# A hybrid attention and mLSTM layer: rotated rows copied from SBUF to SBUF, and two of seven mLSTM operands split as their heads finish

## The reference, cut to what matters

```python
h = rmsnorm(x, norm_w)
q_a, k_a, v_a, z_a, q_m, k_m, v_m, o_m, z_m, g = split(h @ w_in)     # w_in: 2048 x 8208
# group A: 8 heads of 128; QK norm, rotary on the first 32 of 128 head dims,
qa = rope_partial(rmsnorm(q_a, q_norm_w)); ka = rope_partial(rmsnorm(k_a, k_norm_w))
# three (window, dilation) patterns, mixed by their softmax denominators
attn = mix(dilated_attention(qa, ka, va)) * silu(z_a)
# group B: 4 heads (qk 128, v 256), bidirectional chunked mLSTM
hm = rmsnorm(mlstm(qm, km, vm) + flip(mlstm(flip(...))), m_norm_w)
hm = sigmoid(o_m) * hm * silu(z_m)
y = x + concat([attn, hm]) @ w_out                                    # w_out: 2048 x 2048
```

## Time and profile before

| | us |
|---|---|
| median of 3 runs | 1972.75 |
| lowest, highest | 1968.98, 1974.37 |
| profiled execution | 1969.88 |
| its span, first to last instruction | 1968.1 |
| PE busy | 1920.2 (98% of the span) |
| DVE busy | 1354.8 (69%) |
| ACT busy | 896.3 (46%) |
| POOL busy | 226.5 (12%) |

### The profile page before, as it was taken

One profiled execution on the slowest core, in us unless ns is written; L12 is line 12 of the kernel. 1 busy time (PEld: TensorE's weight loads), 2 busy tenths in 40 slices (PEclk: granted clock), 3 DMA queues, 4 the chain that ended last, 5 costly groups with the idle time before them and its releaser, 6 DMA issues.

```text
span 1968.1 us, 26806 instructions
## 1 busy us (share of the span) xinstructions
PE 1920.2 (98%) x8865; PEld 1571.3 (80%) x8865; DVE 1354.8 (69%) x2804; ACT 896.3 (46%) x1494; POOL 226.5 (12%) x244
## 2 busy tenths in 40 slices
PE   8999999999999999999999999999999799999999
PEld 6888887788888888888887878778787687877787
DVE  7677868778768767867866565655665856557655
ACT  6554326335336425434444245546546464455222
POOL 0231000110010010011000211110110111111111
PEclk9999999999999999999999999999999899999999
DMA  6676544564464486366356963563655736447554
GB/s 212 219 266 224 196 143 147 134 149 132 119 164 128 106 230 180 102 147 152 122 190 263 242 162 86 137 162 64 174 120 144 257 75 193 112 108 216 100 120 105
DMA packets 164216, 310.09 MB, mean 158 GB/s; under 512 B 18224, under 2 KB 41408, under 8 KB 160976
## 3 DMA queue, kind: packets, MB, share of 16 engines
q1 hardware_dynamic: 131200, 243.36, 37.8%
q0 software_dynamic: 30720, 57.69, 18.7%
q10 hardware_dynamic: 2160, 7.34, 1.0%
HBM read 202.53 MB, written 122.56 MB: 165 GB/s over the span
## 4 chain that ended last, share of the span: by engine, by line
PE 84%; DMA 6%; issue 4%; DVE 3%; ACT 2%; SPq 0%; POOL 0%; DVEq 0%; ACTq 0%; POOLq 0%
PE ps L870 22%; PE ps L874 21%; PE ps L872 21%; PE ps L1043 3%; PE ps L1072 3%; DMA arena<-rot_dram 2%; DMA rot_dram<-arena 2%; PE ps L1012 1%; PE ps L968 1%; PE ps L977 1%; PE ps L1054 1%; PE ps L971 1%; PE ps L1044 1%; PE ps L889 1%; PE ps L1074 1%
## 5 line engine op out<-in xcount | busy, mean ns | idle before, releaser
L870 PE MATMUL ps<-t_hi,w_hi 128*128 128x512 f32 x2184 | 878.5, 402 | 23.4 <-issue 10.7
L874 PE MATMUL ps<-t_hi,w_lo 128*128 128x512 f32 x2184 | 854.4, 391 | 0.0
L872 PE MATMUL ps<-t_lo,w_hi 128*128 128x512 f32 x2184 | 853.8, 391 | 0.0
L870 PEld LDWEIGHTS ps<-t_hi,w_hi 128*128 128x128 f32 x2184 | 412.1, 189 | 115.9 <-issue 34.5
L874 PEld LDWEIGHTS ps<-t_hi,w_lo 128*128 128x128 f32 x2184 | 411.6, 188 | 88.3
L872 PEld LDWEIGHTS ps<-t_lo,w_hi 128*128 128x128 f32 x2184 | 412.3, 189 | 81.8
L1410 DVE TENSOR_TENSOR w_lo<-s_tmp,w_hi 128x512 fp32r<-128x512 f32 x312 | 221.3, 709 | 183.3 <-ACT w_hi L1109 173.1
L1109 ACT CAST w_hi<-s_tmp 128x512 fp32r<-128x512 f32 x312 | 193.0, 619 | 281.0 <-PE ps L874 263.8
L1410 DVE TENSOR_TENSOR w_lo<-w_raw,w_hi 128x512 fp32r<-128x512 f32 x234 | 165.2, 706 | 152.1 <-ACT w_hi L1109 146.1
L1109 ACT CAST w_hi<-w_raw 128x512 fp32r<-128x512 f32 x234 | 144.8, 619 | 222.1 <-PE ps L874 215.9
L455 POOL DMA_DIRECT2D fin_dram<-xt x32 | 28.1, 877 | 845.4 <-ACT xt L1128 812.6
(11 more groups left out here) (226 smaller groups left out, 2292.4 us busy)
## 6 DMA issues: line engine op xcount, KB each, us to landing
w_raw<-w_all_dram SPq DMA_DIRECT2D x320, 256.0 KB, 4.1
fin_dram<-xt SPq DMA_DIRECT2D x128, 256.0 KB, 4.4
fin_dram<-xt POOLq DMA_DIRECT2D x128, 256.0 KB, 5.5
arena<-fin_dram SPq DMA_DIRECT2D x64, 512.0 KB, 7.6
outT_dram<-xt POOLq DMA_DIRECT2D x60, 256.0 KB, 4.3
arena<-xT_dram SPq DMA_DIRECT2D x44, 256.0 KB, 5.7
arena<-xT_dram SPq DMA_DIRECT2D x16, 512.0 KB, 4.5
outT_dram<-xT_dram SPq DMA_DIRECT2D x16, 512.0 KB, 5.7
```

Of the source, the lines that this page charges most:

```text
L870: nc.tensor.matmul(ps[:, bank, :], hi, t_hi[:, n, k, :], start=new and k == 0, stop=False, skip_group_check=True)
L872: nc.tensor.matmul(ps[:, bank, :], hi, t_lo[:, n, k, :], start=False, stop=False, skip_group_check=True)
L874: mm = nc.tensor.matmul(ps[:, bank, :], lo, t_hi[:, n, k, :], start=False, stop=k == KP - 1, skip_group_check=True)
```

## The change

There are two parts.

**Rotated rows.** POOL's store to and load from `rot_dram` go. SP now copies the rotated rows from `turn` straight into raw q or k, in four transfers of 32 partitions x 256 elements for each of the two, at `at` 5 (q) and 6 (k), ahead of the broadcast of that step. To do so SP waits for DVE's rotation (`a_rot`).

**Two operands split early.** Operands 0 and 2 of the mLSTM half of y are plain blocks: the first 512 columns of heads 0 and 1, and of heads 2 and 3. At `at` 61 of each mLSTM head ACT copies those columns of `gate` to `yk_hi`, at 62 DVE makes `yk_lo`, and at 63 SP stores both in `yk_dram`. They lie where `hbuf` lies, so the next head's first result waits for the store, and the load of block B21 for the border at 329 moves from offset -9 to -4, its scaling on ACT from -5 to 0. At the border at 441 ACT loads both parts of operands 0 and 2 from `yk_dram`, and their two splits are gone; the split of operand 3 moves from offset 8 to 7 and that of 4 from 9 to 8.

```diff
-Y_SPLIT = {3: {3: 0, 5: 1, 6: 2, 8: 3, 9: 4, 10: 5, 11: 6}, 4: {3: 0, 5: 1, 6: 2, 7: 3, 8: 4, 9: 5, 10: 6}}
+Y_SPLIT = {3: {5: 1, 7: 3, 8: 4, 10: 5, 11: 6}, 4: {3: 0, 5: 1, 6: 2, 7: 3, 8: 4, 9: 5, 10: 6}}
+Y_KEPT = (0, 2)
...
+        yk_hi = nc.alloc_sbuf_tensor_at("yk_hi", [P, 2, HALF], F32R, offset=arena_at + 4 * 2048)
+        yk_lo = nc.alloc_sbuf_tensor_at("yk_lo", [P, 2, HALF], F32R, offset=arena_at + 4 * 3072)
...
# SP, loads of the border at 329, and its wait
-                if off == -9 and b == 2:
+                if off == -4 and b == 2:
                     sp.wait_ge(m_htr, 2 * M_HEADS)
+                    sp.wait_ge(yk_out, 32 * M_HEADS)
-                for blk, at in ((B11, -13), (B12, -12), (B22, -11), (B21, -9)):
+                for blk, at in ((B11, -13), (B12, -12), (B22, -11), (B21, -9 if b == 1 else -4)):
...
# SP, mLSTM head j
                 if at == 25:
                     if j > 0:
                         sp.wait_ge(m_out, 16 * j)
+                        sp.wait_ge(yk_split, 2 * j)
...
+                if at == 63:
+                    sp.wait_ge(yk_split, 2 * j + 2)
+                    n, kp = divmod(2 * j, KP)
+                    for part_, src in enumerate((yk_hi, yk_lo)):
+                        sp.dma_start(yk_dram[n, part_][:, kp:kp + 2, :], src[:].bitcast(F32)).then_inc(yk_out, 16)
...
# SP, attention head h
                 if at in (5, 6):
                     i = at - 5
+                    sp.wait_ge(a_rot, 8 * h + 4 * i + 4)
+                    sp.wait_ge(a_sq, 2 * h + 2)
+                    for part_ in range(4):
+                        k, q = divmod(part_, 2)
+                        sp.dma_start((raw_a, raw_b)[i][0:ROT, part_ * 256:(part_ + 1) * 256],
+                                     turn[i][2 * ROT * k + q:2 * ROT * (k + 1):2, 0:256]).then_inc(turned[i], 16)
                     sp.wait_ge(rs_out, 32 * (h + 1))
...
# ACT
-                for blk, at in ((B11, -10), (B12, -9), (B22, -8), (B21, -5)):
+                for blk, at in ((B11, -10), (B12, -9), (B22, -8), (B21, -5 if b == 1 else 0)):
...
+                if at == 61:
+                    act.wait_ge(m_y, 2 * j + 2)
+                    nc.scalar.copy(yk_hi[:], gate.rearrange("p (e t) -> p e t", e=2)[:, :, 0:HALF]).then_inc(yk_split, 1)
...
-                    y_there(act, 3, off - 1)
-                    act.dma_start(t_lo[:, off - 1].bitcast(F32), y_block(3, off - 1)).then_inc(t_in[off - 1], 16)
+                    if off - 1 in Y_KEPT:
+                        act.wait_ge(yk_out, 32 * M_HEADS)
+                        for part_, t in enumerate((t_hi, t_lo)):
+                            act.dma_start(t[:, off - 1].bitcast(F32), yk_dram[Y_KEPT.index(off - 1), part_]
+                                          ).then_inc(t_in[off - 1], 16)
+                    else:
+                        y_there(act, 3, off - 1)
+                        act.dma_start(t_lo[:, off - 1].bitcast(F32), y_block(3, off - 1)).then_inc(t_in[off - 1], 16)
...
# DVE
                     if n == 0 and j > 0:
                         dve.wait_ge(m_htr, 2 * j)
+                        dve.wait_ge(yk_out, 32 * j)
...
+                if at == 62:
+                    dve.wait_ge(yk_split, 2 * j + 1)
+                    nc.vector.tensor_tensor(yk_lo[:], gate.rearrange("p (e t) -> p e t", e=2)[:, :, 0:HALF],
+                                            yk_hi[:].bitcast(F32), ALU.subtract).then_inc(yk_split, 1)
...
-                dve.wait_ge(turned[i], 16 * (h + 1))
+                dve.wait_ge(turned[i], 64 * (h + 1))
...
# POOL: gone
-                    pool.wait_ge(a_rot, 8 * h + 4 * i + 4)
-                    pool.dma_start(rot_dram[h, i], turn[i][:, 0:256]).then_inc(rot_out[i], 16)
...
-                    pool.wait_ge(rot_out[i], 16 * (h + 1))
-                    pool.wait_ge(a_sq, 2 * h + 2)
-                    pool.dma_start(halves((raw_a, raw_b)[i][0:ROT]),
-                                   rot_dram[h, i].rearrange("(s r q) n -> r s (q n)", s=2, q=2)).then_inc(turned[i], 16)
```

More of the change, by code:

```diff
@@ L138 @@
 SUMS = (3, 1, 5, 4)
+Y_KEPT = (0, 2)
 FIRST_SPLIT = (4, 1, 4, 1, 1, 5, 4)
 def t_made(n, b):
-    return FIRST_SPLIT[n] + b - int(b >= 2 and n in KEPT)
+    return FIRST_SPLIT[n] + b - int(b >= 2 and n in KEPT) - int(b >= 3 and n in Y_KEPT)
 def t_loaded(n, b):
-    return 32 * (n in KEPT) + 16 * (b - 2)
+    return 32 * (n in KEPT) + 16 * (b - 2) + 16 * (b >= 3 and n in Y_KEPT)
 def sums_of_y(h):
@@ L168, in prepared_in, with build_program @@
     return u + 2 if u + 2 < UNITS else None
-def build_program(nc, xT, w_all, w_gates, vecs, norm_cols, m_cols, att_mask, rope, eye, tri, fin, xrs_dram, y_dram, t_dram, ty_dram, eps_dram, rows_dram, rs_dram,
-                  rot_dram, outT):
+def build_program(nc, xT, w_all, w_gates, vecs, norm_cols, m_cols, att_mask, rope, eye, tri, fin, xrs_dram, y_dram, t_dram, ty_dram, yk_dram, eps_dram, rows_dram, rs_dram, outT):
     with ExitStack() as ctx:
@@ L377, in build_program @@
         m_out = sem("m_out")
+        yk_split = sem("yk_split")
+        yk_out = sem("yk_out")
         q_raw = sem("q_raw")
@@ L391, in build_program @@
         turn_in = [sem(f"turn_in{i}") for i in range(2)]
-        rot_out = [sem(f"rot_out{i}") for i in range(2)]
         a_rot = sem("a_rot")
@@ L863, in product @@
                     pe.wait_ge(t_in[n], t_loaded(n, 2))
+                elif g == STAGE[3] and n in Y_KEPT:
+                    pe.wait_ge(t_in[n], t_loaded(n, 3))
                 elif g in STAGE:
@@ L2042, in squares @@
                         nc.gpsimd.tensor_tensor(sq_acc, sq_acc, x_ring[:, r % 2, :], ALU.add).then_inc(xg_sum, 1)
-            def turned_rows(h, at):
-                if at in (4, 5):
-                    i = at - 4
-                    pool.wait_ge(a_rot, 8 * h + 4 * i + 4)
-                    pool.dma_start(rot_dram[h, i], turn[i][:, 0:256]).then_inc(rot_out[i], 16)
-                if at in (5, 6):
-                    i = at - 5
-                    pool.wait_ge(rot_out[i], 16 * (h + 1))
-                    pool.wait_ge(a_sq, 2 * h + 2)
-                    pool.dma_start(halves((raw_a, raw_b)[i][0:ROT]),
-                                   rot_dram[h, i].rearrange("(s r q) n -> r s (q n)", s=2, q=2)).then_inc(turned[i], 16)
             def add_ym(u):
@@ L2072, in _ @@
                 added(*divmod(u, PRODUCTS))
-                for h in range(ATT_HEADS):
-                    turned_rows(h, u - A_START[h])
                 add_ym(u)
@@ L2188 @@
     rs_dram = nc.dram_tensor("rs_dram", (ATT_HEADS, 2, TB, P), _mybir.dt.float32, kind="Internal").ap()
-    rot_dram = nc.dram_tensor("rot_dram", (ATT_HEADS, 2, P, 256), _mybir.dt.float32, kind="Internal").ap()
     eps_dram = nc.dram_tensor("eps_dram", (2 * TB, P), _mybir.dt.float32, kind="Internal").ap()
@@ L2193 @@
     ty_dram = nc.dram_tensor("ty_dram", (2, len(SUMS), P, KP, HALF), _mybir.dt.float32, kind="Internal").ap()
+    yk_dram = nc.dram_tensor("yk_dram", (len(Y_KEPT), 2, P, KP, HALF), _mybir.dt.float32, kind="Internal").ap()
     outT = nc.dram_tensor("outT_dram", (O_TILES, P, SEQ), _mybir.dt.float32, kind="ExternalOutput").ap()
-    build_program(nc, *args, fin, xrs_dram, y_dram, t_dram, ty_dram, eps_dram, rows_dram, rs_dram, rot_dram, outT)
+    build_program(nc, *args, fin, xrs_dram, y_dram, t_dram, ty_dram, yk_dram, eps_dram, rows_dram, rs_dram, outT)
     r = _run(nc, [arrays], core_ids=[0])
```

## The result

The changed kernel takes 1980.72 us (median of 20 runs, 1973.49 to 1986.43), the kernel before 1974.38 us in the same comparison (20 runs, 1968.55 to 1986.56). The ratio is 1.0026, with a 95% interval of 1.0014 to 1.0038: slower by about 5 us (2.8 to 7.5). Forecast were 1963.7 us and a range of 1956 to 1971; the time is outside it and on the other side of before.

The account below looks back on a forecast made before the run. PE was taken as the bound, busy 1920.2 of 1968.1 us, with gains only where it waits. The terms -6.6 - 3.4 + 0 + 0.3 + 0.6 = -9.1 us took 1972.75 to 1963.7 us, range 1956 to 1971.

Parts of the forecast that it names:

- The other edits: Step pricing mLSTM's added copy and subtraction at 0.3 us, and the border at 329 at +0.6 us.
- bound of 4.9 us: Upper limit for the mLSTM work: the time each of DVE and ACT would add if nothing hid it.
- signs of being wrong: Listed observations that would refute the forecast, among them new PE waits at the last steps of an mLSTM head.
- The border at 441: Removing operand 2's split resumes PE 2.3 us earlier, but the gain moves to another wait: 0, bounds -4 and +3.
- upper bound of +3: At the border at 441, operand 2's second megabyte delays the broadcast in a crowded stretch; 1 MB is 2.9 us.
- what is late next?: Question at the border at 441, answered by head 5's broadcast: issued no earlier, with four copies now before it.
- The rotated rows: Attention heads: an 8.9 us path after rotation replaces POOL's round trip, saving 6.6 us of waits and 3.4 of clock.
- two clock windows: After the waits of heads 0 and 7, PE's full clock returns: 2 x 1.7 = 3.4 us saved.
- Rival 1: Attention heads: copies ahead cost the broadcast 2 us of landing; only -2.0 us in all, 1970.7 us; chance 0.21.
- The rule of turns between queues: On SP: DMA engines take queues in turn, so copies ahead in its queue make the broadcast land later; no separate size.
- The border at 329: B21's four scalings, 2.56 us on ACT, now just before the first cast: +0.6 us, bounds 0 and 2.6.
- Rival 2: Attention heads: broadcast landings of 9.8 us become the rule, making it 22.9 us slower, 1995.6 us; chance 0.07.

Follow-up runs that it names:

- ym_late: Changed kernel with the first three steps of the copies of y moved from units 226, 231, 236 to 246, 251, 256; 1967.91 us, 0.9993 of before.
- store_late: Changed kernel with head 1's store of kept parts moved from step 63 to 68, behind head 2's k and q loads; 1969.16 us, 0.9990 of before.
- border_thin: ym_late with all but 64 columns of operand 2's low part not loaded at the border at 441; 1965.49 us, 0.9965 of before.
- rot_only: Kernel before with only the rotated rows moved to SP, no operands kept; 1966.24 us, 0.9981 of before.
- rot_swap: rot_only with SP issuing each step's broadcast ahead of the four copies; 1960.37 us, 0.9954 of before; repeated, 1960.18 us, 0.9935.
- store_act: Changed kernel with all four heads' stores of kept parts issued by ACT instead of SP at step 63; 1977.84 us, 1.0019 of before.

## Why the prediction was wrong

**The step that failed: "The other edits".** It put the mLSTM work at 0.3 us, as work "beside products on which PE does not wait", and the next head's result at "nine products behind it: nothing". I priced the copy and the subtraction, which indeed cost nothing (1.05 us on ACT and 1.22 us on DVE a head, and nobody is shown waiting for them), and let the step's two DMAs stand for free. They are 1 MB a head in SP's queue. Of head 1 they stand one microsecond ahead of 2 MB of copies and 7 us ahead of the loads of k and q, which had landed 1.4 us late already. That row (L957, 1.37 us) was in the trace before, in the list of PE's waits as the sixth line; I hadn't followed it. The cost is 9.2 us between units 220 and 260. Of that 6.9 is wait (8.30 - 1.37). The rest is clock, by an estimate from the windows: 0.56 and 0.93 make some 10 us at 1.2 GHz, of which about 4.7 fall behind PE's restart at 736.67, and these cost 2.4. Head 3 adds up to 1.7. Its bound of 4.9 us came from engine time and so couldn't hold it. Among the signs of being wrong I had named new waits at the last steps of an mLSTM head; the wait came where the next head needs its loads. That the loss takes both the store and the copies is shown by ym_late and store_late.

**The border at 441: 0 forecast, +3.3 found.** The upper bound of +3 named the right cause, a second megabyte in a crowd, but had it delay the broadcast. What it delayed stands ahead of the split: the load of q's rotary rows, for which DVE waited 2.58 us where it had waited 0.62, and the load of the sums, 12.0 us against 6.1. So PE never got the 2.3 us that the missing split was to give; the forecast's "what is late next?" had looked behind the split only. border_thin shows the megabyte as the cause.

**The rotated rows: -6.6 and -3.4 forecast.** The mechanism was right, the size was not. In the seven heads besides head 5 PE's waits before the scores fell from 8.2 to 5.0 us, by 3.2 and not by 6.6; the 0.7 of head 5 went as well. Of the two clock windows one came back: after head 0 the window has 1.00, after head 7 it is still 0.83 (in rot_only both show 1.00).

```profile
1170.00:1180.00 10.00, 9.09 (x41) 6.70 (x40) 5.68 (x15) 4.74 (x12) 0.86 (x1) 1.00 0.96 324
...
1740.00:1750.00 10.00, 9.77 (x39) 7.52 (x40) 6.03 (x22) 4.77 (x9) 0.86 (x1) 0.83 0.31 64
```

Source views of the copies and of k's broadcast in after:

```profile
L699 SPq DMA_DIRECT2D arena<-arena x64: 462/594/1720, 1157.9 to 1728.9; - x64
...
DMA to landing us min/median/max: 1.8/3.3/9.6
```

```profile
L708 SPq DMA_DIRECT2D arena<-rs_dram x16: 469/526/543, 1163.9 to 1730.2; - x16
...
  DVE arena L1842: 10.9, 7
...
DMA to landing us min/median/max: 3.9/5.0/7.4
```

The issue of one copy is 0.594 us in the median, as estimated from the earlier trace rows. The landing of 5.0 is the median over both broadcasts of all heads, and the sum needed that of the second of each pair, which it took as 6.0. That one landed in 4.6 to 5.9 us in five heads and in 7.1, 7.1 and 7.4 in heads 0, 2 and 7. In head 7 the four copies took 3.45 us besides, so that the path was 11.6 us and not 8.9: 1.2 more of issue and 1.4 more of landing. In head 0 it was 10.2, nearly all of the excess landing. In heads 3 and 5 the last broadcast was issued 6.7 and 7.4 us after the rotation, since SP reached the step late. DVE waited for the broadcast in seven heads, 10.9 us together. Rival 1 (the broadcast takes the place of the round trip) thus held in head 7 and in part in head 0, and head 3 was late for another reason; the forecast held or nearly held in heads 1, 2, 4 and 6, with waits of 0 to 0.7 us. Rot_only's 0.19%, about 4 us, is between the two: 10 us were forecast for this part, 2.9 by the rival without its 0.9 of other edits.

**The rule of turns between queues.** The Trainium skill, "DMA: Bandwidth & Descriptors", section "Queues, rings and completion order", says that each DMA engine takes its queues in turn, packet by packet. I drew from it that the broadcast lands later behind copies in its own queue. The medians over all heads don't show it: 5.0 us in after and 5.2 in rot_swap, where the copies stand behind, against 5.6 in the earlier trace rows. Single heads do. The pair of head 0, in before (L690 at 1146.7) and in after (L708 at 1163.9):

```profile
DMA to landing us min/median/max: 4.5/4.9/5.4
```

```profile
DMA to landing us min/median/max: 6.1/6.6/7.1
```

The second of the pair takes 7.1 us in heads 0 and 2 in both after and rot_only, and 5.4 and 4.9 in before, 5.4 and 4.1 in rot_swap. Heads 1 and 4 show nothing of the kind (5.9 and 4.6 in after, 6.1 and 5.8 in before). But behind the copies the broadcast is also issued later, with three loads of weights right behind it (at 1165.10 in head 0, against 1163.95 for the broadcast). So the trace agrees in some heads, and whether the copies ahead or the loads behind delay it isn't shown.

**The border at 329: +0.6 forecast.** PE's wait of 0.58 us became 0.89, in every kernel with the late B21 and in none without. Right in sign and small; a wait of 0.35 two products on went with it, and the stretch from 325 to 357 is no longer than before (89.8 us against 90.0). The wait for the loads from `t_dram` some products on moves between nothing and 3.3 us, in kernels without an edit there too (2.2 in rot_swap), and isn't counted.

**Rival 2** did not occur: no broadcast of k took over 7.4 us in after. The slower result came by a way that no rival named.

## What to carry to other kernels

Price the DMAs of an edit apart from its instructions: for each, list what is issued in the same crowd within some 10 us and read for every such load the landing against the first use; one that is already waited for, by however little, has no slack to give. Engine time saved at a place where transfers are dense is worth little if the loads beside it land just in time: at the border at 441 the sums had 0.4 us of slack, and a split of 2.3 us that was gone brought about 1 us even in border_thin, and a loss with the second megabyte. And where an issuer works in order, the transfer that needs nothing goes ahead of the one that waits.

## What the runs showed of the hardware

- The same 512 KB load took 7.7, 9.3, 11.4 and 15.8 us to land (ym_late, before, store_act, after), in kernels that differ in what was issued in the 10 us ahead of it. SP's issue of the next load, of q, was 0.41 or 0.42 us in the first three and 3.81 in the last.
- A copy of 32 KB inside SBUF was no cheaper to issue than the load of 512 KB (0.38 us in before): 0.594 us in the median and up to 1.72. It landed in 1.8 to 9.6 us. The two stores of 512 KB landed in 3.0 and 5.0 us when ACT issued them, 2.8 us earlier, and from SP in 7.5 and 10.2 with the copies behind them (after) and 6.9 and 8.1 without (ym_late).
- Of TensorE's clock: around PE's wait of 8.30 us the windows show 0.56 and 0.93, around waits of 2.30 us (after) and 2.19 us (head 2 of rot_swap) 0.83, and around waits of 2.00 us (head 2 of store_late) and 0.91 us (after) 1.00.
